# All activations begin 64 bytes further on in each partition

## The chip, the cores and the metric

The kernel runs on 1 core of a Trainium2 chip. Its time is the device time of that core in microseconds, the median of several runs. Each core has a matrix engine (TensorE, in the profile PE, with its weight loads as PEld), a vector engine (DVE), a scalar engine (ACT), GpSimd (POOL) and a queue engine (SP), with one on-chip memory of 128 partitions between them.

## The reference

Two blocks follow each other on 256 tokens of width 2048. What matters here is that nearly all of it is products of activations with large weight matrices, in float32:

```python
def first_block(...):                      # two layers
    xm_l = x_lat * (1.0 + sc_l) + sh_l     # shift and scale from a small product with cond
    proj = xm @ w_in                       # layer 0: q, k, v, o, z_m, gates, u_p, z_p
    ...                                    # mLSTM scan, pooling
    x_lat = layer_norm(ALPHA * x_lat + g_l * (y_l @ w_out_even[j]), ...)
    u, v, z = jnp.split(xm @ w_in, 3, axis=-1)      # layer 1, and y_l @ w_out_odd

def second_block(...):
    c_q, c_kv, k_r, x_r, y_r, ga, gr = split_columns(n @ w_in[l])
    ...                                    # attention, recurrent branch, each with its output product
    h = h + (g_attn * y_attn + g_rnn * y_rnn) @ w_out[l]
    h = h + peer_ffn(...)                  # 16,384 experts
    gate = jax.nn.sigmoid(rms_norm(h, ple_norm[l]) @ w_ple_gate[l])
    h = h + gate * (p[l] @ w_ple_proj[l])
    return rms_norm(h, final_norm)
```

The experts (`peer_u`, `peer_v`, 16,384 x 2048 each) are not gathered: the kernel multiplies with all of them and picks by one-hot products.

## The kernel before, in words

All weights stream from memory in 669 units of 128 partitions x 2048 floats (8 KB in each partition) through a ring of four buffers. ACT rounds each half of a unit to the reduced form fp32r (`unit_hi`, line 1102); POOL (line 478), or DVE in some stages (lines 1659, 1775, 2414), writes the rest, ring minus `unit_hi`, to `unit_lo`. The activations are split in the same way into a hi and a lo tile (`xl`, `xc`, `y`, `cn`, `o`, `ry`, `mix`, `w_r`, `p_r`). A product is then three matmuls: weights hi with activation hi, weights hi with activation lo, weights lo with activation hi.

Most of them stand in `n_unit` (line 541): the stationary operand is a 128x128 piece of a unit's half, the moving operand 256 columns of one activation tile. The same triple stands in `two_units` (513), for both sets of tokens (696), in the experts' second product (1055, activations `w_r`) and in the last projection (1078). In `v1_tokens` (593) and `o_tokens` (570) the roles are exchanged: 128 columns of the activation are stationary, 512 columns of a unit's half move. In lines 673 and 675, too, a unit's half moves, against a stationary operand of only 4 or 2 columns (`cond_parts`).

The chip's own scheduling sets no order here: every engine runs a program written by hand, with semaphores between them. SP loads units in order, each when its ring buffer is free. ACT, then POOL or DVE, then PE follow at most four halves apart (`NBUF = 4`).

On-chip memory is laid out by hand as well. First come, one behind the other and each rounded up to 64 bytes, the fixed tiles: the ring, four `unit_hi`, four `unit_lo` of 4,096 bytes in each partition, the residual `h`, vectors, constants (`con`), rows. Ahead of the zones they take 91,584 bytes from the first, `base0`. Everything else is placed by `zone(name, kb, ...)` at `z0` plus a number of KB: all the split activations, and nearly all other intermediate tiles. A few zones lie 64 bytes or a multiple of that beside a whole KB (`q0` at 98.0625 KB and `u_pad`'s neighbours at 106.0625 KB among them). The change is in the line that sets `z0`.

The operand addresses that follow, modulo 512 bytes and counted from `base0`: every buffer of the weights' halves starts at 0, and every 128-column piece of it too. The split activations start at 448. `con` starts at 320.

Of the kernel before, what the change touches and what calls it, by code (L numbers as in the profile page):

```python
# [190 lines left out]
def program(nc, A, out):  # L191
    with ExitStack() as ctx:
        base0 = (nc.sbuf_base + 63) // 64 * 64
        at = [base0]
# [4 lines left out]
        def fixed(name, shape, dt):  # L199
            t = place(name, shape, dt, at[0])  # L200
            at[0] += (int(np.prod(shape[1:])) * 4 + 63) // 64 * 64
            return t
# [12 lines left out]
        rstd = fixed("rstd", [P, T], F32)  # L215
        tick = fixed("tick", [1, 1], F32)
        lam_s = fixed("lam_s", [P, KC], F32)
        z0 = (at[0] + 63) // 64 * 64
        KB = 1024

        def zone(name, kb, shape, dt=F32):
# [2559 lines left out]
```

## Time and profile before

| | |
|---|---|
| median of 3 runs | 3753.03 us (3751.19 to 3781.72) |
| the profiled execution's own time | 3763.23 us |
| its span, first to last instruction | 3761.4 us |
| PE busy | 3610.3 us, 96% of the span |
| PEld busy | 3481.5 us, 93% |
| DVE, POOL, ACT busy | 2091.6, 2039.0, 1562.3 us |
| granted TensorE clock, mean | 0.98 |

The profiled execution is 10.2 us above the median of the runs and inside their spread. A busy PE says only that some matmul was in the array: the next one is fed before the last one has left, so that one lasts about 276 ns while a new one begins every 113 ns. How fast PE goes is read from the distance of the starts: first and last start of a group, divided by the number of matmuls between them.

### The profile page before, as it was taken

To read this page: it belongs to the slowest core of one execution; us is meant where nothing else is said; L and a number is where in the kernel's file an instruction comes from. 1 tells how busy PE (TensorE), PEld (TensorE's weight loads), DVE (VectorE), ACT (ScalarE), POOL (GpSimd) and SP (SyncE) were. 2 spreads that over 40 slices of the span, in tenths; PEclk is the share of its full clock that TensorE was granted. 3 is DMA by queue.
4 is the path that set the end of the run, shared out by engine and by line. 5 is a ranking of instruction groups with operands and counts; after the bars stand their busy time and mean duration, and the time that the engine had idled before them with its cause. 6 is when DMAs were issued, how large, how long until landed. Compare 5 with 4: busy or idle time off the path is not lost.

```text
span 3761.4 us, 71588 instructions
## 1 busy us (share of the span) xinstructions
PE 3610.3 (96%) x30016; PEld 3481.5 (93%) x30016; DVE 2091.6 (56%) x3062; ACT 1562.3 (42%) x1970; POOL 2039.0 (54%) x816
## 2 busy tenths in 40 slices
PE   6999998999999889999999999999999999999998
PEld 3799897979999879999999999999999999999998
DVE  6686456783724465554114679784444666544454
ACT  5413433334344334454444434434444444444453
POOL 0147591008084648789899960007888100188876
PEclk9999999999999999999999999999999999999999
DMA  8557751765653424545455545545555455455543
GB/s 330 191 210 261 277 221 73 299 234 189 251 200 132 147 100 157 180 157 185 175 200 192 192 182 185 179 169 184 196 190 192 179 179 183 180 196 190 192 166 124
DMA packets 98407, 716.37 MB, mean 190 GB/s; under 512 B 11040, under 2 KB 11168, under 8 KB 12064
## 3 DMA queue, kind: packets, MB, share of 16 engines
q1 hardware_dynamic: 97056, 703.65, 51.0%
q10 hardware_dynamic: 1152, 9.87, 0.7%
q8 instruction: 148, 2.42, 0.3%
q14 instruction: 51, 0.42, 0.0%
HBM read 711.38 MB, written 2.10 MB: 190 GB/s over the span
## 4 chain that ended last, share of the span: by engine, by line
PE 83%; DVE 8%; POOL 4%; DMA 2%; ACT 2%; issue 2%; DVEq 0%; SPq 0%; POOLq 0%; ACTq 0%
PE bank L541 54%; PE bank L1055 19%; POOL unit_lo L478 3%; DMA ring<-in_w 2%; PE bank L593 2%; PE bank L696 2%; DVE unit_lo L1775 1%; PE bank L570 1%; PE bank L1006 1%; ACT unit_hi L1102 1%; PE bank L635 1%; PE bank L513 1%; DVE ada_acc L1576 1%; PE bank L805 1%; DVE unit_lo L1659 1%
## 5 line engine op out<-in xcount | busy, mean ns | idle before, releaser
L478 POOL TENSOR_TENSOR unit_lo<-ring,unit_hi 128x1024 fp32r<-128x1024 f32 x806 | 2023.2, 2525 | 1656.7 <-ACT unit_hi L1102 1655.2
L1102 ACT ACTIVATE unit_hi<-ring 128x1024 fp32r<-128x1024 f32 x1204 | 1239.7, 1056 | 1194.7 <-PE bank L541 479.5
L541 PE MATMUL bank<-xl_hi,unit_hi 128*128 128x256 f32 x4688 | 1321.6, 282 | 23.2 <-POOL unit_lo L478 9.9
L541 PE MATMUL bank<-xl_lo,unit_hi 128*128 128x256 f32 x4688 | 1307.5, 279 | 0.0
L541 PE MATMUL bank<-xl_hi,unit_lo 128*128 128x256 f32 x4688 | 1307.0, 279 | 0.0
L541 PEld LDWEIGHTS bank<-xl_hi,unit_hi 128*128 128x128 f32 x4688 | 890.5, 190 | 30.5 <-issue 11.5
L541 PEld LDWEIGHTS bank<-xl_hi,unit_lo 128*128 128x128 f32 x4688 | 888.0, 189 | 0.0
L541 PEld LDWEIGHTS bank<-xl_lo,unit_hi 128*128 128x128 f32 x4688 | 886.8, 189 | 0.6
L1055 PE MATMUL bank<-w_r,unit_hi 128*128 128x256 f32 x4096 | 699.7, 277 | 4.0 <-DVE w_r L2584 4.0
L1055 PEld LDWEIGHTS bank<-w_r,unit_hi 128*128 128x128 f32 x4096 | 619.1, 188 | 4.3 <-issue 4.3
L1055 PE MATMUL bank<-w_r,unit_lo 128*128 128x256 f32 x2048 | 566.8, 277 | 0.0
L2584 DVE TENSOR_TENSOR w_r<-peer_w,w_r 128x256 fp32r<-128x256 f32 x128 | 290.0, 2266 | 398.2 <-ACT w_r L1471 397.6
L1055 PEld LDWEIGHTS bank<-w_r,unit_lo 128*128 128x128 f32 x2048 | 386.0, 188 | 0.0
L2414 DVE TENSOR_TENSOR unit_lo<-ring,unit_hi 128x1024 fp32r<-128x1024 f32 x224 | 265.4, 1220 | 54.9 <-ACT unit_hi L1102 54.6
L1576 DVE SCALAR_TENSOR_TENSOR ada_acc<-ring,cond,ada_acc 128x2048 f32<-128x2048 f32 x64 | 185.5, 2899 | 29.7 <-DMA ring<-in_w 28.7
L1659 DVE TENSOR_TENSOR unit_lo<-ring,unit_hi 128x1024 fp32r<-128x1024 f32 x102 | 120.5, 1221 | 72.6 <-ACT unit_hi L1102 58.5
L1452 ACT ACTIVATE peer_w<-bank 128x248 f32<-128x248 f32 (+30 forms) x87 | 24.3, 279 | 304.4 <-PE bank L541 304.4
L541 PE MATMUL bank<-ry_hi,unit_hi 128*128 128x256 f32 x480 | 132.8, 277 | 0.6 <-issue 0.6
L541 PE MATMUL bank<-ry_lo,unit_hi 128*128 128x256 f32 x480 | 132.5, 276 | 0.0
L541 PE MATMUL bank<-ry_hi,unit_lo 128*128 128x256 f32 x480 | 132.5, 276 | 0.0
L541 PE MATMUL bank<-xc_hi,unit_hi 128*128 128x256 f32 x448 | 126.3, 282 | 0.6 <-ACT ple_in L1495 0.6
L541 PE MATMUL bank<-xc_lo,unit_hi 128*128 128x256 f32 x448 | 125.7, 281 | 0.0
(441 smaller groups left out, 5135.0 us busy)
## 6 DMA issues: line engine op xcount, KB each, us to landing
ring<-in_w SPq DMA_DIRECT2D x669, 1024.0 KB, 4.8
resid<-in_xT ACTq DMA_DIRECT2D x1, 2048.0 KB, 15.7
tmp_ctx<-in_ctxT ACTq DMA_DIRECT2D x1, 2048.0 KB, 11.3
sgu_rows<-in_sgr ACTq DMA_DIRECT2D x1, 2048.0 KB, 9.5
rnn_gates<-in_rgw ACTq DMA_DIRECT2D x1, 2048.0 KB, 8.8
out<-resid SPq DMA_DIRECT2D x4, 512.0 KB, 2.6
con<-in_con ACTq DMA_DIRECT2D x1, 512.0 KB, 3.3
con<-in_con ACTq DMA_DIRECT2D x1, 448.0 KB, 7.9
```

Source lines behind the costliest of these rows:

```text
L478: pool.tensor_tensor(lb[b][:], ring[slot][:, f * HALF:(f + 1) * HALF], hb[b][:].bitcast(F32), ALU.subtract).then_inc(lo_done, 1)
L513: mm = pe.matmul(bank[(s.t0 + j) % TILES][:, 0:T], w[b][:, (k % 8) * P:(k % 8 + 1) * P], mv[x][:, k, :], start=(k == 0 and w is hb and x = ...
L541: mm = pe.matmul(bank[(s.t0 + tile[m]) % TILES][:, 0:T], w[b][:, (i % 8) * P:(i % 8 + 1) * P], mv[x][:, k, :], start=(k == 0 and w is hb a ...
L570: mm = pe.matmul(bank[(s.t0 + 2 * (j // 4) + t) % TILES][:], xl[x][:, k, t * P:(t + 1) * P], w_[u][:, q * 512:(q + 1) * 512], start=(k == ...
L593: mm = pe.matmul(bank[(s.t0 + 2 * block + t) % TILES][:], xl[x][:, k, t * P:(t + 1) * P], w_[u][:, q * 512:(q + 1) * 512], start=(k == 0 a ...
L696: mm = pe.matmul(dst[:, m * T:(m + 1) * T], w_[b][:, (i % 8) * P:(i % 8 + 1) * P], mv[x][:, k, :], start=(first and w_ is w[0] and x == 0 ...
L1055: mm = pe.matmul(o, w_[b][:, c * P:(c + 1) * P], wr[j % 2][:, x, :], start=(first and j == 0 and cc % 2 == 0 and w_ is hb and x == 0), sto ...
L1102: act.activation(hb[b][:], ring[slot][:, f * HALF:(f + 1) * HALF], ACT.Copy).then_inc(hi_done, 1)
L1576: dve.scalar_tensor_tensor(a[:], ring[u % RING][:], col, a[:], ALU.mult, ALU.add).then_inc(plain_done, 1)
L1659: dve.tensor_tensor(lb[b][:], ring[(s.u0 + s.npos[j]) % RING][:, f * HALF:(f + 1) * HALF], hb[b][:].bitcast(F32), ALU.subtract).then_inc(l ...
L2414: dve.tensor_tensor(lb[b][:], ring[(s.u0 + u) % RING][:, f * HALF:(f + 1) * HALF], hb[b][:].bitcast(F32), ALU.subtract).then_inc(lo_done, 1)
L2584: dve.tensor_tensor(wr[j % 2][:, 1, :], at(W, i), wr[j % 2][:, 0, :].bitcast(F32), ALU.subtract).then_inc(S("wr_ready"), 1)
```

## The change

`z0`, the place from which all zones are counted, was rounded up to 64 bytes. It is now rounded up to a multiple of 512 bytes counted from `base0`. By the sizes of the fixed tiles, 91,584 becomes 91,648 bytes from `base0`: 64 bytes further. Every zone moves by these 64 bytes; rings, halves of units, residual, vectors and constants stay. No instruction, wait or order is changed.

```diff
         tick = fixed("tick", [1, 1], F32)
         lam_s = fixed("lam_s", [P, KC], F32)
-        z0 = (at[0] + 63) // 64 * 64
+        z0 = (at[0] - base0 + 511) // 512 * 512 + base0
         KB = 1024
 
         def zone(name, kb, shape, dt=F32):
             off = z0 + int(kb * KB)
```

## Rows read from the trace of the kernel before

**Rows 1.** The page: busy time, share of the span, instructions of each engine.

```profile
PE 3610.3 (96%) x30016; PEld 3481.5 (93%) x30016; DVE 2091.6 (56%) x3062; ACT 1562.3 (42%) x1970; POOL 2039.0 (54%) x816
```

**Rows 2.** The page: shares of the chain that ended last, by engine and by line.

```profile
PE 83%; DVE 8%; POOL 4%; DMA 2%; ACT 2%; issue 2%; DVEq 0%; SPq 0%; POOLq 0%; ACTq 0%
PE bank L541 54%; PE bank L1055 19%; POOL unit_lo L478 3%; DMA ring<-in_w 2%; PE bank L593 2%; PE bank L696 2%; DVE unit_lo L1775 1%; PE bank L570 1%; PE bank L1006 1%; ACT unit_hi L1102 1%; PE bank L635 1%; PE bank L513 1%; DVE ada_acc L1576 1%; PE bank L805 1%; DVE unit_lo L1659 1%
```

**Rows 3.** PE's groups by line and form: busy us, mean ns of one, idle before.

```profile
L541 PE MATMUL bank<-xl_hi,unit_hi 128*128 128x256 f32 x4688 | 1321.6, 282 | 23.2 <-POOL unit_lo L478 9.9 <-DVE unit_lo L1659 5.4 <-issue 2.8
...
L1055 PE MATMUL bank<-w_r,unit_hi 128*128 128x256 f32 x4096 | 699.7, 277 | 4.0 <-DVE w_r L2584 4.0
L1055 PE MATMUL bank<-w_r,unit_lo 128*128 128x256 f32 x2048 | 566.8, 277 | 0.0
...
L541 PE MATMUL bank<-xc_hi,unit_hi 128*128 128x256 f32 x448 | 126.3, 282 | 0.6 <-ACT ple_in L1495 0.6
```

**Rows 4.** Line 1055, window 2600:2700: ns min/median/max, first and last start.

```profile
L1055 PE MATMUL bank<-w_r,unit_hi x589: 276/276/276, 2599.9 to 2699.9; 128*128 128x256 f32 x197
L1055 PE MATMUL bank<-w_r,unit_lo x295: 276/276/276, 2599.8 to 2699.8; 128*128 128x256 f32 x148
```

**Rows 5.** Line 541, window 2240:2340, the same columns.

```profile
L541 PE MATMUL bank<-xl_lo,unit_hi x284: 281/281/281, 2239.8 to 2339.8; 128*128 128x256 f32 x142
L541 PE MATMUL bank<-xl_hi,unit_lo x284: 281/281/281, 2240.0 to 2339.9; 128*128 128x256 f32 x142
L541 PE MATMUL bank<-xl_hi,unit_hi x283: 281/281/281, 2240.1 to 2339.7; 128*128 128x256 f32 x142
```

**Rows 6.** PE in order of time about 2380: start us, us, what.

```profile
2379.28 0.28 PE L541 MATMUL bank<-xl_hi,unit_hi 128*128 128x256 f32 x1
2379.40 0.28 PE L541 MATMUL bank<-xl_lo,unit_hi 128*128 128x256 f32 x1
2379.52 0.28 PE L541 MATMUL bank<-xl_hi,unit_lo 128*128 128x256 f32 x1
2379.64 0.82 PE L988 MATMUL bank<-con,peer_g 128*128 128x128 f32 x6
2380.21 0.37 PE L541 MATMUL bank<-xl_hi,unit_hi 128*128 128x256 f32 x1
...
2380.77 0.28 PE L541 MATMUL bank<-xl_lo,unit_hi 128*128 128x256 f32 x1
2380.88 0.28 PE L541 MATMUL bank<-xl_hi,unit_lo 128*128 128x256 f32 x1
2380.99 0.28 PE L541 MATMUL bank<-xl_hi,unit_hi 128*128 128x256 f32 x1
```

**Rows 7.** Line 541 in seven stretches: window, length, PE busy, clock, DMA.

```profile
333.20:376.00 42.80, 42.80 (x366) 1.00 0.59 222
...
1732.20:1811.00 78.80, 78.80 (x671) 1.00 0.54 193
2176.10:2379.00 202.90, 202.89 (x1723) 1.00 0.53 192
3658.80:3743.00 84.20, 84.20 (x717) 1.00 0.38 137
sum 498.20, PE 498.19; mean PE 71.17
```

**Rows 8.** Line 593, window 800:840; columns as in rows 4.

```profile
L593 PE MATMUL bank<-unit_hi,xl_lo x59: 388/388/394, 799.7 to 839.5; 128*128 128x512 f32 x59
L593 PE MATMUL bank<-unit_lo,xl_hi x59: 392/392/394, 799.9 to 839.8; 128*128 128x512 f32 x59
L593 PE MATMUL bank<-unit_hi,xl_hi x58: 388/390/392, 800.4 to 839.1; 128*128 128x512 f32 x58
```

**Rows 9.** Lines 673 and 675 in order of time, columns as in rows 6.

```profile
81.36 0.39 PE L673 MATMUL bank<-unit_hi,cond_parts 128*4 128x512 f32 x1
...
82.98 0.39 PE L675 MATMUL bank<-unit_lo,cond_parts 128*2 128x512 f32 x1
```

**Rows 10.** Plain f32 matmuls of lines 635, 652 and 958, windows of 25, 8, 1 us.

```profile
L635 PE MATMUL bank<-ln_sq,con x32: 379/379/379, 743.1 to 749.8; 128*128 128x256 f32 x32
...
L652 PE MATMUL bank<-con x38: 379/379/379, 750.0 to 758.0; 128*128 128x256 f32 x38
...
L958 PE MATMUL bank<-x_conv,rnn_gates x4: 377/378/379, 1542.1 to 1542.7; 128*128 128x256 f32 x4
```

**Rows 11.** Every engine in two stretches: PE, PEld, DVE, ACT, POOL, clock, DMA.

```profile
2240.00:2340.00 100.00, 100.00 (x851) 100.00 (x851) 92.74 (x172) 40.20 (x52) 0.00 (x0) 1.00 0.53 189
2600.00:2700.00 100.00, 100.00 (x884) 100.00 (x884) 42.80 (x19) 44.58 (x56) 88.18 (x38) 1.00 0.54 197
```

## The prediction

> **What bounds the kernel now.** I read the engines' shares first: PE is busy 96% of the span, DVE 56%, POOL 54%, ACT 42% [rows 1]. The chain of waits agrees: 83% of it is PE, 54% of the span in line 541 and 19% in line 1055 [rows 2]. Both lines feed 256 columns of a split activation against a 128x128 piece of a unit's half. PE hardly waits: the 4,688 matmuls of the first group have 23.2 us of idle time before them in all [rows 3]. So the time is the number of these matmuls times the distance of their starts. In the profile's list by line and form, line 541 has three groups for each activation, with 4,688, 480, 448, 272, 256, 256 and 224 matmuls each: 3 x 6,624 = 19,872. Line 1055 has 4,096 + 2,048 = 6,144 [rows 3]. Together 26,016. One nanosecond more or less for each is 26 us, 0.7%.
>
> **Two distances.** In the window from 2600, line 1055 begins 884 matmuls from 2599.8 to 2699.9: 100.1 / 883 = 113.4 ns [rows 4]. In the window from 2240, line 541 begins 851 from 2239.8 to 2339.9: 100.1 / 850 = 117.8 ns, and each one lasts 281 instead of 276 ns [rows 5]. The granted clock is 1.00, the 2.4 GHz level, in both [rows 11], so it isn't the clock. Nor is it the operands: about 2380 the same line with the same tiles changes from 0.12 us to 0.11 us a step, with six f32 matmuls of line 988 between [rows 6]. The long distance is a way in which the stream settles after an interruption, and stays. It fills seven long stretches of 498.2 us in sum [rows 7]; shorter ones I leave out. At the short distance these would take 498.2 x (1 - 113.4/117.8) = 18.6 us less.
>
> At one column for each cycle of 2.4 GHz, 256 columns take 106.7 ns. Something therefore adds 6.7 ns to a matmul at the short distance and 11.1 ns at the long one, in all about 6.7 x 26,016 + 18.6 = 193 us. That is what a better place of the operands could win at the very most, and the question of this change.
>
> **The change part by part.** It removes and adds no instruction, on no engine or queue. It moves every zone by 64 bytes. For a matmul of line 541 or 1055 the moving operand starts at 448 modulo 512 bytes from the weights' halves before, and at 0 after; its stationary operand stays at 0. What that costs no row shows directly, so I bound it by the nearest ones.
>
> - A moving operand that starts at 0 is there already: in line 593 a unit's half moves, 512 columns of it. 176 matmuls begin from 799.7 to 839.8: 40.1 / 175 = 229 ns, 114.6 ns for 256 columns [rows 8]. That lies between the two distances of line 541. Starting the moving stream on the 512-byte multiple wins nothing there.
> - The fetch of the stationary operand doesn't cause the stall: with 4 or 2 stationary columns the eight matmuls of lines 673 and 675 begin from 81.36 to 82.98, 1.62 / 7 = 231 ns apart for 512 columns [rows 9], as slow as with 128. A collision between the two fetches, which is what their relative place would set, should be far smaller there.
> - Two operands at the same place modulo 512 are there too, in plain f32. Line 652 takes both from `con` (difference 0), 8.0 / 37 = 216 ns apart; line 958 takes both from zones a whole number of KB apart (difference 0), 0.6 / 3 = 0.20 us with one digit; line 635 has 128 bytes of difference, 6.7 / 31 = 216 ns [rows 10]. No difference between 0 and 128. But f32 needs 216 ns for its 256 columns, so that its fetch has more time than that of fp32r.
>
> So the three rows that come nearest all say: no change. From both sides: below, the stall could go down by a step as large as the one between the two distances (4.4 ns), above it could grow by one. 4.4 x 26,016 = 114.5 us. I take 0, because rows 8 have fp32r, the place after the change and the same speed, and keep both ends for the range.
>
> The Trainium skill, "SBUF — State Buffer", section "Who interferes with whom", has TensorE with one read port for the moving operand and one for weight loads, independent of each other and of all engines; by that rule a relative place costs nothing, and the sum stays at 0. Its "Specifications (TRN2)" give lines of 16 bytes, which a shift of 64 leaves as they were. The rule "Back-to-back issue gap" in "TensorE: Matmul & The Clock Gate" gives N/2.4 + 2.5 = 109.2 ns for 256 columns. The trace disagrees: it shows 113.4 ns; by the rule, a stall of 4.2 ns is there to be removed, which would be 109 us.
>
> The other engines: the zones' 64 bytes also move what ACT, DVE and POOL write and read. The split of a unit (ring, `unit_hi`, `unit_lo`) doesn't move, and that is POOL's and most of ACT's work. POOL, 88% busy in the experts' second product, and DVE, 93% in the stretch from 2240 [rows 11], are covered by a PE that is full in both. I cost them at nothing. If PE went to 109.0 ns, POOL would be at 88.2 x 113.4 / 109.0 = 92%: still cover, but little in it. Five DMAs go into zones, against 669 into the ring.
>
> **Sum:** 3763.2 + 0. The profiled execution is 10.2 us above the median of the runs, so the forecast for the median is 3753 us. How often the stream settles at the long distance is chance in part: none of these stretches would take 18.6 us off, twice as many would add as much. The likeliest case's own range is 3725 to 3785.
>
> **The rivals.**
> - *A collision: slower.* Both fetches now start on the same multiple of 512 bytes. If the memory is laid out in banks that repeat with 512 bytes, the load of the next weights and the moving stream ask for the same bank, and the long distance becomes the only one. Place: every triple of lines 541 and 1055. Price: 114.5 for one step more on all, less the 18.6 already paid: +96, 3849 us for the median. It decides from 1.5 ns a matmul on (38 us). For it: that there are two levels at all, with the same operands, tells of something that two streams share. Against it: rows 8 to 10. Chance 0.18, and 0.04 for other losses, of a smaller or a larger step.
> - *The stall goes: faster.* If the stall comes from the difference of 64 bytes between the two operands (448 against 0), equal places take it away: 109.0 instead of 113.4 ns, and no long stretches. -114.5 - 18.6 = -133, 3620 us for the median. For it: line 593 also has a difference of 64 bytes, the other way, and stalls as well; f32 with differences of 0 and 128 doesn't show one. Against it: lines 673 and 675 stall with `cond_parts`, whose pieces start 16 bytes apart and so at many differences. Chance 0.17, and 0.05 for half of that, 3686 us.
> - *The long stretches alone vanish:* -18.6, 3734 us. Inside 1%. Chance 0.10.
> - *The change doesn't do what it says:* if `base0` itself isn't at a multiple of 512, the zones are aligned with the units but not in absolute terms. Then only the relative place has changed, and if the absolute one is what counts, the effect is as good as any other shift of 64 bytes. I count it in the forecast.
>
> **How the numbers follow.** Forecast (no change) 0.46, long stretches gone 0.10; together 0.56 within 1%. One per cent, 37.5 us, is about what a measurement of this kernel tells from no change. Faster by over 1%: 0.17 + 0.05 = 0.22. Slower by over 1%: 0.18 + 0.04 = 0.22. The range goes from 3650, which takes in half a step down but leaves out the whole one, to 3855, which takes in the whole step up: 0.17 below and about 0.02 above are left out. The likeliest time stays 3753.
>
> **What would show it.** If I am right, line 1055 in the experts' second product still begins every 113.4 ns and lasts 276 ns, line 541 shows 113.4 and 117.8 in other stretches, line 593 still takes 229 ns. A collision would show 281 ns or more in line 1055, where there is not one such matmul in rows 4 now. A stall that goes would show distances near 109 ns and a POOL above 90% there. Wrong from the start would be the use of line 593 as a measure for line 541, if the two read the memory in different ways, and the belief that ACT's, DVE's and POOL's work on zones doesn't feel the place.

## The result, and the profile after

The changed kernel takes 3887.78 us (median of 4 runs, 3886.17 to 3888.91) against 3763.3 us for the kernel before (median of 4 runs, the three of the table above and one more; 3751.19 to 3781.72): ratio 1.0326, 95% interval 1.0275 to 1.0377. It is slower by 3.3%, and the forecast of no change and its range (3650 to 3855) are both missed. The spans of the profiled executions are 3887.1 and 3761.4 us, 125.7 us apart.

The page after, engines first, then PE's groups in the columns of [rows 3]:

```profile
PE 3744.4 (96%) x30016; PEld 3620.4 (93%) x30016; DVE 2058.8 (53%) x3062; ACT 1559.7 (40%) x1970; POOL 2029.4 (52%) x816
...
L541 PE MATMUL bank<-xl_hi,unit_hi 128*128 128x256 f32 x4688 | 1343.9, 287 | 16.1 <-POOL unit_lo L478 5.4
L541 PE MATMUL bank<-xl_lo,unit_hi 128*128 128x256 f32 x4688 | 1331.7, 284 | 0.0
```

```profile
L1055 PE MATMUL bank<-w_r,unit_hi 128*128 128x256 f32 x4096 | 738.9, 283 | 4.0 <-DVE w_r L2584 4.0
L1055 PE MATMUL bank<-w_r,unit_lo 128*128 128x256 f32 x2048 | 580.5, 283 | 0.0
```

PE is busy 134.1 us longer with the same 30,016 instructions and idle 8.4 us less (142.7 against 151.1): 125.7, the whole difference. DVE, ACT and POOL are busy no longer than before, against [rows 1]. Line 1055's matmuls last 283 ns where they lasted 277.

The distance of the starts, line 1055 in the window 2650:2750, line 541 in 2300:2380, then line 635 (f32), then line 593 in 820:849; columns as in [rows 4]:

```profile
L1055 PE MATMUL bank<-w_r,unit_hi x557: 280/283/287, 2649.8 to 2749.9; 128*128 128x256 f32 x186
L1055 PE MATMUL bank<-w_r,unit_lo x278: 280/283/287, 2649.9 to 2749.7; 128*128 128x256 f32 x139
```

```profile
L541 PE MATMUL bank<-xl_hi,unit_hi x223: 283/283/283, 2299.8 to 2379.7; 128*128 128x256 f32 x112
L541 PE MATMUL bank<-xl_lo,unit_hi x223: 283/283/283, 2299.9 to 2379.8; 128*128 128x256 f32 x112
L541 PE MATMUL bank<-xl_hi,unit_lo x223: 283/283/283, 2300.0 to 2379.9; 128*128 128x256 f32 x112
```

```profile
L635 PE MATMUL bank<-ln_sq,con x32: 379/379/379, 754.0 to 760.7; 128*128 128x256 f32 x32
```

```profile
L593 PE MATMUL bank<-unit_hi,xl_lo x44: 389/389/389, 819.9 to 848.7; 128*128 128x512 f32 x44
L593 PE MATMUL bank<-unit_hi,xl_hi x43: 389/389/389, 819.6 to 848.2; 128*128 128x512 f32 x43
L593 PE MATMUL bank<-unit_lo,xl_hi x43: 389/389/389, 820.3 to 848.9; 128*128 128x512 f32 x43
```

Line 1055: 835 matmuls in 100.1 us, 100.1 / 834 = 120.0 ns, where [rows 4] have 113.4. Line 541: 669 matmuls in 80.1 us, 80.1 / 668 = 119.9 ns, where [rows 5] have 117.8 and [rows 4], for the same form, 113.4. Line 635: 6.7 / 31 = 216 ns, as in [rows 10]. Line 593: 130 matmuls in 29.3 us, 29.3 / 129 = 227 ns against 229 in [rows 8]: with the roles exchanged and 512 columns, the new place is a little better.

Line 541 and all other engines, in the columns of [rows 11]:

```profile
2300.00:2400.00 100.00, 100.00 (x836) 100.00 (x835) 91.40 (x165) 41.29 (x54) 0.00 (x0) 1.00 0.50 178
2650.00:2750.00 100.00, 100.00 (x835) 100.00 (x835) 40.05 (x18) 42.51 (x53) 83.25 (x36) 1.00 0.53 187
```

The granted clock is 1.00 as before, and in both stretches 835 or 836 matmuls fit where 851 and 884 did. PE is full in both; nobody keeps it waiting there. The fp32r matmuls of 256 columns have become slower by themselves, and the two distances of before have become one of 120 ns.

### The profile page after: what moved, and what is told of

It reads as the page before. It is cut to its first block, busy times and chain, and to the rows that moved or that the text cites. A ratio compares the mean times of both kernels' runs of the same rounds, so it can differ in the third digit from the quotient of the medians.

```text
span 3887.1 us, 71588 instructions
## 1 busy us (share of the span) xinstructions
PE 3744.4 (96%) x30016; PEld 3620.4 (93%) x30016; DVE 2058.8 (53%) x3062; ACT 1559.7 (40%) x1970; POOL 2029.4 (52%) x816
## 4 chain that ended last, share of the span: by engine, by line
PE 83%; DVE 9%; POOL 3%; DMA 2%; ACT 2%; issue 1%; SPq 0%; DVEq 0%; POOLq 0%; ACTq 0%
PE bank L541 54%; PE bank L1055 19%; POOL unit_lo L478 3%; DMA ring<-in_w 2%; PE bank L593 2%; PE bank L696 2%; DVE ada_acc L1576 1%; DVE unit_lo L1775 1%; PE bank L570 1%; PE bank L1006 1%; ACT unit_hi L1102 1%; PE bank L513 1%; PE bank L635 1%; DVE unit_lo L1659 1%; PE bank L805 0%
## 5 line engine op out<-in xcount | busy, mean ns | idle before, releaser
L541 PE MATMUL bank<-xl_hi,unit_hi 128*128 128x256 f32 x4688 | 1343.9, 287 | 16.1 <-POOL unit_lo L478 5.4
L541 PE MATMUL bank<-xl_lo,unit_hi 128*128 128x256 f32 x4688 | 1331.7, 284 | 0.0
L541 PE MATMUL bank<-xl_hi,unit_lo 128*128 128x256 f32 x4688 | 1331.4, 284 | 0.0
L541 PEld LDWEIGHTS bank<-xl_hi,unit_hi 128*128 128x128 f32 x4688 | 904.7, 193 | 22.4 <-issue 10.8
L541 PEld LDWEIGHTS bank<-xl_lo,unit_hi 128*128 128x128 f32 x4688 | 904.9, 193 | 0.5
L541 PEld LDWEIGHTS bank<-xl_hi,unit_lo 128*128 128x128 f32 x4688 | 904.4, 193 | 0.0
L1055 PE MATMUL bank<-w_r,unit_hi 128*128 128x256 f32 x4096 | 738.9, 283 | 4.0 <-DVE w_r L2584 4.0
L1055 PEld LDWEIGHTS bank<-w_r,unit_hi 128*128 128x128 f32 x4096 | 636.7, 191 | 4.3 <-issue 4.3
L1055 PE MATMUL bank<-w_r,unit_lo 128*128 128x256 f32 x2048 | 580.5, 283 | 0.0
```

The lines of the kernel that those rows point to most:

```text
L541: mm = pe.matmul(bank[(s.t0 + tile[m]) % TILES][:, 0:T], w[b][:, (i % 8) * P:(i % 8 + 1) * P], mv[x][:, k, :], start=(k == 0 and w is hb a ...
L1055: mm = pe.matmul(o, w_[b][:, c * P:(c + 1) * P], wr[j % 2][:, x, :], start=(first and j == 0 and cc % 2 == 0 and w_ is hb and x == 0), sto ...
```

## The experiments

Below, *difference* is the start of the moving operand less that of the stationary one in line 1055 and 541, modulo 512 bytes: 448 before, 0 after. e1, e2, e3 and g1 are medians of several executions; all others are single ones, set beside the kernel before on the same chip. Executions of the kernel before go from 3747 to 3805 us, so the single ones are judged by the distance in line 1055, not by the time. Where no other window is named it is 2650:2750, and the rows' columns are those of [rows 4].

**Is it the activations' own place, or the place relative to the weights?** Three kernels. In e1 and e2 `h` and small fixed tiles are taken from behind the halves and put ahead of `unit_hi`, which moves the halves (`vec` and `con` move too); in e3 only the two `w_r` move:

```diff
 e1_units448 (activations stay, halves move: difference 0)
         ring = [fixed(f"ring{i}", [P, UNIT], F32) for i in range(RING)]
+        h = fixed("resid", [P, KC, T], F32)
+        mod = fixed("mod", [P, 96, 2], F32)
+        cond = fixed("cond", [P, KC, 2], F32)
+        tick = fixed("tick", [1, 1], F32)
         hb = [fixed(f"unit_hi{i}", [P, HALF], F32R) for i in range(NBUF)]
 e2_both64 (h and tick ahead of the halves, and:)
+        z0 = (at[0] + 63) // 64 * 64 + 64
 e3_wr64
-        wr = [zone(f"w_r{i}", 100 + 2 * i, [P, 2, T], F32R) for i in range(2)]
+        wr = [zone(f"w_r{i}", 100.0625 + 2 * i, [P, 2, T], F32R) for i in range(2)]
```

> All activations stay where they are in the kernel before; instead the eight buffers of the weights' halves (unit_hi, unit_lo) lie 448 bytes further modulo 512, so that moving and stationary operand of lines 541 and 1055 again start at the same place modulo 512. Theory R (the place of the moving operand relative to the stationary one counts): starts 120.0 ns apart in lines 541 and 1055, no 113.4, line 593 near 227 ns, about 3885 us. Theory A (the moving operand's own place counts): the activations haven't moved, so 113.4 and 117.8 ns as before, 3750 to 3785 us. Theory O (ACT, DVE and POOL are slower on the moved zones): as A.

> Activations 64 bytes further as in the change, and the weights' halves 64 bytes further too: the difference of the two is 448 modulo 512 as in the kernel before, the activations' own place is that of the change. Theory R: 113.4 and 117.8 ns, 3750 to 3785 us. Theory A: 120.0 ns, about 3888 us. Theory O: about 3888 us, with 113.4 ns in line 1055 and the time lost elsewhere.

> Kernel before, with only the two buffers w_r (the moving operand of line 1055, 6144 matmuls) 64 bytes further. Theories R and A: line 1055 goes from 113.4 to 120.0 ns, everything else keeps 113.4 and 117.8; 6144 x 6.6 ns = 40.6 us more, about 3800 us. Theory O: line 1055 keeps 113.4 ns and the time stays within 10 us of before.

- e1: 3896.2 us, ratio 1.0324 (1.0279 to 1.0369). The activations lie where they lay, and the whole loss is there.
- e2: 3762.35 us, ratio 0.9999 (0.9971 to 1.0026). The activations lie where the change put them, and nothing is lost.
- e3: 3802.01 us, ratio 1.0089 (1.0058 to 1.012), 36 us over the 3765.83 of before in the same job, where 40.6 were expected from line 1055 alone.

Line 1055 in e1, e2, e3:

```profile
L1055 PE MATMUL bank<-w_r,unit_hi x557: 283/283/283, 2649.8 to 2749.9; 128*128 128x256 f32 x186
L1055 PE MATMUL bank<-w_r,unit_lo x278: 283/283/283, 2650.1 to 2749.8; 128*128 128x256 f32 x139
```

```profile
L1055 PE MATMUL bank<-w_r,unit_hi x589: 276/276/276, 2649.8 to 2749.8; 128*128 128x256 f32 x197
L1055 PE MATMUL bank<-w_r,unit_lo x295: 276/276/276, 2649.9 to 2749.9; 128*128 128x256 f32 x148
```

```profile
L1055 PE MATMUL bank<-w_r,unit_hi x557: 283/283/283, 2649.8 to 2749.9; 128*128 128x256 f32 x186
L1055 PE MATMUL bank<-w_r,unit_lo x278: 283/283/283, 2649.9 to 2749.6; 128*128 128x256 f32 x139
```

120.0 ns (100.1 / 834), 113.4 ns (100.1 / 883), 120.0 ns. The relative place decides; theories A and O are out.

**Which differences are good?** The halves moved by other amounts, activations as before (e4 to e8: `h` and tiles of 64, 128, 192, 256 and 320 bytes modulo 512 ahead of `unit_hi`), and two with steps of 32 bytes:

```diff
 e4_units64                      e5_units128
+        tick = fixed(...)       +        cond = fixed(...)
 e6_units192                     e7_units256
+        cond = ..., tick = ...  +        mod = fixed(...)
 e8_units320                     e11_zones32
+        mod = ..., tick = ...   +        z0 = (at[0] + 63) // 64 * 64 + 32
 e12_diff160 (cond ahead of the halves, and:)
+        z0 = (at[0] + 63) // 64 * 64 + 96
```

> The weights' halves 64 bytes further, activations as before: the moving operand starts at 384 modulo 512 from the stationary one, a place that no run has shown. Theory R with a bank that repeats every 512 bytes: the distance is one of a small set (109, 113.4, 117.8, 120.0 ns), not that of before in all stretches; if two fetches only collide when they start together, 113.4 or less everywhere, 3740 us or less. Theory A: 113.4 and 117.8 as before.

> The weights' halves 128 bytes further, activations as before: the moving operand starts at 320 modulo 512 from the stationary one. So far 448 gives 113.3 and 117.8 ns (114.7 ns in the mean), 0 gives 120.0 and 384 gives 118.8 in the mean. Theory R1 (the two fetches go round the same banks of 64 bytes with a period of 512; the weight load begins late and half-way through the moving stream, and only some differences let both pass): the mean here differs from 118.8 and 114.7 by over 1 ns. Theory R2 (448 is a special place since there the moving stream is one bank behind; all others collide): about 119 to 120 ns, 3855 to 3890 us.

> The weights' halves 192 bytes further: difference 256 modulo 512, half the supposed period, farthest from the start of the other fetch. Theory R1: a different distance again, perhaps the lowest, since the fetches of a period of 512 are farthest apart here (109 to 113.4 ns, 3630 to 3750 us). Theory R2: 119 to 120 ns, 3855 to 3890 us. If the period is 256 instead of 512, the same as difference 0: 120.0 ns and 3890 us.

> The weights' halves 256 bytes further: difference 192 modulo 512. Theory R1: its own distance. With a period of 256 the same as 448: 113.3 and 117.8 ns and 3750 to 3785 us. Theory R2: 119 to 120 ns, 3855 to 3890 us.

> The weights' halves 320 bytes further: difference 128 modulo 512. Theory R1: its own distance. With a period of 256 the same as 384: 118.8 ns and 3855 us. With a period of 128 the same as 0: 120.0 ns and 3890 us. Theory R2: 119 to 120 ns, 3855 to 3890 us.

> Kernel before with all zones only 32 bytes further: difference 480, 224 modulo 256, between 192 (113.3 and 117.8 ns) and 0 (120.0 ns). If banks are 64 bytes wide, half of each piece is in the next bank: a distance between 114 and 120 ns, 3760 to 3890 us. If 32 bytes shift the stream in time by half a bank, a distance outside the set so far (for example 116.7 or 110 ns).

> Weights' halves 128 bytes and zones 96 bytes further: difference 416, 160 modulo 256, between 128 (118.7 ns) and 192 (113.3 and 117.8 ns). If 192 is the middle of a good region, about 113 to 118 ns and 3740 to 3850 us; if it is the region's edge on this side and 224 is good, this one is near 118.7 ns. Faster than before only if the settled distance falls below 113.3 ns or the 117.8 ns stretches vanish: 3740 us or less.

| run | difference | modulo 256 | line 1055, ns | time, us (before on the same chip) |
|---|---|---|---|---|
| after | 0 | 0 | 120.0 | 3887.78 (3763.3) |
| e6 | 256 | 0 | 120.0 | 3893.59 (3780.14) |
| e5 | 320 | 64 | 117.8 | 3832.07 (3780.14) |
| e4 | 384 | 128 | 118.6 | 3854.92 (3765.83) |
| e8 | 128 | 128 | 118.6 | 3854.66 (3780.14) |
| e12 | 416 | 160 | 118.6 | 3853.55 (3804.97) |
| before | 448 | 192 | 113.4 | |
| e7 | 192 | 192 | 113.4 | 3748.44 (3780.14) |
| e11 | 480 | 224 | 118.3 | 3849.22 (3804.97) |

In the last column before is a single execution, but for the first row and e4, where it is a median. Two pairs and the place of before repeat with 256 bytes, to the digit of the view. The rows of e5, e7 and e6 are the pattern:

```profile
L1055 PE MATMUL bank<-w_r,unit_hi x568: 279/279/279, 2649.8 to 2749.9; 128*128 128x256 f32 x190
L1055 PE MATMUL bank<-w_r,unit_lo x283: 280/280/280, 2650.1 to 2749.7; 128*128 128x256 f32 x142
```

```profile
L1055 PE MATMUL bank<-w_r,unit_hi x590: 276/276/276, 2649.9 to 2750.0; 128*128 128x256 f32 x197
L1055 PE MATMUL bank<-w_r,unit_lo x295: 276/276/276, 2649.8 to 2749.7; 128*128 128x256 f32 x148
```

```profile
L1055 PE MATMUL bank<-w_r,unit_hi x557: 283/283/283, 2649.8 to 2749.9; 128*128 128x256 f32 x186
L1055 PE MATMUL bank<-w_r,unit_lo x278: 283/283/283, 2650.0 to 2749.8; 128*128 128x256 f32 x139
```

Of the six places tried modulo 256 only 192 gives 113.4 ns; 32 bytes to either side cost 5 ns. The kernel before had the good one. That e6, half of 512 away, might be best was wrong: it is the changed kernel again. R1's period was wrong (256, not 512), and R2 fails by e7, which is as good as before, and by e5 (117.8 ns, 3832 us, where it said 119 to 120). e12 came out at what had been named for 192 as the edge of a good region, but by e11 that region doesn't go on to 224: 192 is good by itself.

The table is of line 1055, and 192 isn't the only place with more than one distance. In e12 line 541 goes at two within 100 us, at the same clock (windows 2040:2080 and 2140:2180, columns as in [rows 11]):

```profile
2040.00:2080.00 40.00, 40.00 (x336) 40.00 (x335) 16.96 (x38) 16.43 (x17) 36.27 (x16) 1.00 0.55 195
2140.00:2180.00 40.00, 40.00 (x343) 40.00 (x343) 32.12 (x24) 17.14 (x17) 39.49 (x16) 1.00 0.58 207
```

That is 120.0 and 117.5 ns by the starts; e4's line 541 has stretches at 118.7 and at 120.0 ns. Line 593, with the roles exchanged, answers to the place in another way: here e5 with its 126 matmuls in 29.2 us (29.2 / 125 = 234 ns, against 229 before and 227 after):

```profile
L593 PE MATMUL bank<-unit_hi,xl_hi x42: 393/396/398, 819.7 to 848.0; 128*128 128x512 f32 x42
L593 PE MATMUL bank<-unit_hi,xl_lo x42: 393/396/398, 820.2 to 848.4; 128*128 128x512 f32 x42
L593 PE MATMUL bank<-unit_lo,xl_hi x42: 393/396/398, 820.7 to 848.9; 128*128 128x512 f32 x42
```

**Does the size of the weight load matter?** Line 1055 with fewer stationary columns:

```diff
 e9_thin_448, e10_thin_0 (e10 and f4 with z0 64 bytes further)
-  mm = pe.matmul(o, w_[b][:, c * P:(c + 1) * P], wr[j % 2][:, x, :],
+  mm = pe.matmul(o[0:4, :], w_[b][:, c * P:c * P + 4], wr[j % 2][:, x, :],
 f4_m64_0
+  mm = pe.matmul(o[0:64, :], w_[b][:, c * P:c * P + 64], wr[j % 2][:, x, :],
```

> The kernel before (difference 448, which the runs so far show to be the same as 192 modulo 256), with only 4 instead of 128 stationary columns in line 1055: the weight load shrinks, the moving stream stays. 124 of 128 columns of the experts' second product are left out. If the two fetches collide, line 1055 no longer depends on the place: the same distance as in the next run, 109 to 114 ns. If the moving stream alone is limited, 113.3 ns stay.

> The changed kernel (difference 0) with the same 4 stationary columns in line 1055, with 124 of 128 columns of that product left out. Collision of the two fetches: line 1055 falls from 120.0 ns to that of the run before this one (109 to 114 ns), about 40 us less than 3888. If the weight load has no part in it, 120.0 ns stay.

> The changed kernel (difference 0) with 64 instead of 128 stationary columns in line 1055, half of the columns of that product are left out. 128 columns gave 120.0 ns, 4 columns 113.3 ns. If the loss grows with the length of the weight load: about 116.7 ns. If one meeting of the two fetches is enough: 120.0 ns. If only the load's end matters, 113.3 ns.

Line 1055 in e9, e10, f4:

```profile
L1055 PE MATMUL bank<-w_r,unit_hi x572: 277/278/279, 2649.9 to 2749.8; 128*4 128x256 f32 x191
L1055 PE MATMUL bank<-w_r,unit_lo x287: 277/279/279, 2649.8 to 2749.9; 128*4 128x256 f32 x144
```

```profile
L1055 PE MATMUL bank<-w_r,unit_hi x590: 276/276/276, 2649.8 to 2750.0; 128*4 128x256 f32 x197
L1055 PE MATMUL bank<-w_r,unit_lo x295: 276/276/276, 2649.9 to 2749.9; 128*4 128x256 f32 x148
```

```profile
L1055 PE MATMUL bank<-w_r,unit_hi x590: 276/276/276, 2649.7 to 2749.8; 128*64 128x256 f32 x197
L1055 PE MATMUL bank<-w_r,unit_lo x295: 276/276/276, 2650.0 to 2749.9; 128*64 128x256 f32 x148
```

At difference 0, 64 columns and 4 columns (both 100.2 / 884 = 113.3 ns) take the loss away; 128 columns have it. At 448, 4 columns cost 100.1 / 858 = 116.7 ns, more than 128 do. A plain collision, where less to load is never worse, doesn't give that. The times were 3775.91 us (e9) and 3842.4 us (e10), with 3804.97 for before on that chip, and 3846.1 us (f4), with 3767.74.

So the number of stationary columns counts, and by e1 and e2 the place of the stationary operand does. Whether it is the second half of the load that does the harm at difference 0 isn't shown: with fewer stationary columns the output has fewer partitions too (`o[0:64]`, `o[0:4]`), and no run changes one without the other. Line 1055 loses 6,144 x 6.6 = 41 us at difference 0 and line 541 most of the rest; the fewer columns were tried in line 1055 alone, and line 541 stayed at 120.0 ns in e10 and f4.

**Does each matmul answer to the load beside it?** Only `unit_lo` moved, `cond` or `tick` or both put between `unit_hi` and `unit_lo` (with this `h`, `vec` and `con` move by as much):

```diff
         hb = [fixed(f"unit_hi{i}", [P, HALF], F32R) for i in range(NBUF)]
+        cond = fixed("cond", [P, KC, 2], F32)      # f2, g1; tick: f1; both: f3
         lb = [fixed(f"unit_lo{i}", [P, HALF], F32R) for i in range(NBUF)]
```

> Only unit_lo lies 64 bytes further: difference 448 for the two matmuls with unit_hi, 384 (128 modulo 256) for the one with unit_lo. Theory N (a moving stream collides with the load of the next weights, which runs beside it): only the start behind xl_lo x unit_hi moves away, the two others keep 113.3 ns; mean (2 x 113.3 + 118.7) / 3 = 115.1 ns. Theory M (the three streams settle together): all three distances change, mean not 115.1. The 117.8 ns stretches stay in both. About 3770 to 3830 us. A version without any 117.8 ns would be faster than before: 3735 us.

> Only unit_lo lies 128 bytes further: difference 320 (64 modulo 256) for the matmul with unit_lo. Theory N: mean (2 x 113.3 + 117.8) / 3 = 114.8 ns, the long step behind xl_lo x unit_hi. Theory M: another mean, all three steps changed. About 3770 to 3830 us; faster than before only if the 117.8 ns stretches go.

> Only unit_lo lies 192 bytes further: difference 256 (0 modulo 256) for the matmul with unit_lo. Theory N: mean (2 x 113.3 + 120.0) / 3 = 115.6 ns with 120.0 only behind xl_lo x unit_hi, about 3790 us. If its own weights count instead of the next ones, 120.0 only behind xl_hi x unit_lo. Theory M: another mean.

> The arrangement of f2 (unit_lo alone 128 bytes further, everything else as before) timed against the kernel before. If its single time of 3733 us was no accident, the median is 3725 to 3740 us, 0.5 to 1.2% below before, with less spread than before, since the stretches at 117.8 ns, whose number changes from run to run, are gone. If it was chance (a run with few such stretches), the median is 3750 to 3770.

Line 1055 in f1, f2, f3:

```profile
L1055 PE MATMUL bank<-w_r,unit_hi x566: 279/282/286, 2649.8 to 2750.0; 128*128 128x256 f32 x189
L1055 PE MATMUL bank<-w_r,unit_lo x282: 277/280/281, 2650.1 to 2749.7; 128*128 128x256 f32 x141
```

```profile
L1055 PE MATMUL bank<-w_r,unit_hi x590: 276/276/276, 2649.9 to 2750.0; 128*128 128x256 f32 x197
L1055 PE MATMUL bank<-w_r,unit_lo x295: 276/276/276, 2649.8 to 2749.8; 128*128 128x256 f32 x148
```

```profile
L1055 PE MATMUL bank<-w_r,unit_hi x547: 282/283/290, 2649.8 to 2749.9; 128*128 128x256 f32 x183
L1055 PE MATMUL bank<-w_r,unit_lo x273: 282/283/283, 2650.0 to 2749.8; 128*128 128x256 f32 x137
```

118.3, 113.3 and 122.2 ns, where theory N said 115.1, 114.8 and 115.6. For f3 the 122.2 ns are only the first of the two rounds of line 1055; in the second, from 3378 us on, it goes at 117.8 (windows 2650:2750 and 3550:3650, columns as in [rows 11]):

```profile
2650.00:2750.00 100.00, 100.00 (x820) 100.00 (x819) 40.38 (x18) 41.54 (x52) 83.57 (x35) 1.00 0.50 178
3550.00:3650.00 100.00, 100.00 (x851) 100.00 (x850) 41.68 (x18) 43.10 (x54) 86.74 (x36) 1.00 0.52 188
```

N falls in all three, by either value of f3. In the window from 2650 the three steps of a triple, by the starts in the trace, are about 116, 119 and 120 ns in f1 and 118, 122 and 127 ns in f3, against 113 to 114 before: all three change there, as theory M said, though `unit_lo` alone has moved. In f2 none changes (113 to 114), which M did not say either. So the triple doesn't come apart into three independent pairs; M names that and doesn't forecast a distance. The times of f1 and f3 were 3839.15 and 3873.18 us, both above what had been expected. f2 took 3732.67 us against 3767.74, below what had been expected. Timed, g1 takes **3736.26 us** (11 runs, 3731.93 to 3739.8) against 3762.66 (16 runs, 3747.45 to 3801.11): ratio 0.9914, 0.9885 to 0.9942. Its page and line 541 in 2200:2280:

```profile
PE 3583.0 (96%) x30016; PEld 3454.4 (92%) x30016; DVE 2094.2 (56%) x3062; ACT 1561.8 (42%) x1970; POOL 2042.5 (55%) x816
...
L541 PE MATMUL bank<-xl_lo,unit_hi 128*128 128x256 f32 x4688 | 1302.0, 278 | 0.0
```

```profile
L541 PE MATMUL bank<-xl_hi,unit_lo x231: 275/277/284, 2199.8 to 2279.9; 128*128 128x256 f32 x116
L541 PE MATMUL bank<-xl_hi,unit_hi x230: 275/277/384, 2199.9 to 2279.7; 128*128 128x256 f32 x115
```

In that stage, where [rows 5] last 281 ns, they now last 277. PE is busy 27.3 us less than before; the prediction had reckoned 18.6 us for the seven long stretches and left out the shorter ones. By 0.9%, with an interval that leaves out 1, g1 is faster than the kernel before.

## Why the prediction was wrong, point by point

- **What bounds the kernel** was right: 26,016 matmuls, a nanosecond of each worth 26 us, and all that changed is that distance. 6.6 x 26,016 = 171.7 us less the 27.3 us which the long stretches had cost before (by g1) gives 144.4; PE is busy 134.1 longer. Added up from the starts in the two traces, line 541 takes 99.8 us more and line 1055 39.2; what makes up the rest isn't resolved. PE's idle time became 8.4 us shorter.
- **The step that failed** is "A moving operand that starts at 0 is there already", line 593 as the measure for the change, and with it the 0 in the sum. Line 593's moving operand starts at 0, but its stationary one started at 448: its difference was 64, not 0. The prediction knew this difference, for it counts it in favour of its rival of a stall that goes, and didn't apply it here. By e1 and e2 the moving operand's own start has no effect, so rows 8 said nothing on difference 0. What stood there in place of the 0 was 6.6 ns for each matmul: 120.0 ns in line 1055 instead of 113.4. There was no row with fp32r and difference 0, and the sum should have said so. In line 593 itself, with roles and columns exchanged, the effect even has the other sign: 229 to 227 ns.
- **"The fetch of the stationary operand doesn't cause the stall"**, from 4 and 2 columns in [rows 9], was wrong as an inference. e1 and e2 show that the stationary operand's place has its part, e10 that with 4 columns the loss at difference 0 is gone, and e9 that 4 columns are slower than 128 at 448, for a reason that stays open. A slow stream with a small load doesn't acquit the large one.
- **The f32 rows** [rows 10] were read rightly and don't carry over: 216 ns before and after. The prediction named the doubt, that f32 has more time, and gave it too little weight.
- **The other engines at nothing**: right. DVE, ACT and POOL are busy as long or less, and e2 has the new place of all zones at a ratio of 0.9999. For the ports between engines, as the Trainium skill has them in "SBUF — State Buffer", "Who interferes with whom", that is no contradiction. The word "independent", which it has for TensorE's own two read ports, doesn't hold as the prediction used it: by that rule e1 should have cost nothing, and it cost 3.2%. The 109.2 ns from "TensorE: Matmul & The Clock Gate", "Back-to-back issue gap", in the Trainium skill, were reached by no arrangement; the shortest fp32r distance that any run settled at is 113.3 ns. The prediction used that formula wrongly: the section gives it for an isolated matmul and says that in a stream of loads and matmuls both set the spacing. A stall of 4.2 ns "by the rule" doesn't follow from it.
- **The rival of the collision** had the place and the sign, at 0.18. Its size was too small: I took the step between the two distances of before (4.4 ns) for the next one, and it was 6.6 ns from the short one, where 113.4 became 120.0 and not 117.8. Its 3849 us would have been 3753 + 171.7 - 18.6 = 3906, the measured time is 3888, and the range ended at 3855. Its period of 512 bytes is 256, and a plain collision isn't the mechanism.
- **The stall goes** (3620 us) happened nowhere. **The long stretches vanish** happened, in g1, through another place, and was worth 0.9% (0.6 to 1.2%), somewhat more than the 18.6 us, 0.5%, put on it.

What stays open is how the fetches share the memory: why the loss at difference 0 needs more than 64 stationary columns, why 4 columns are worse than 128 at 448, what sets the several distances of one place, and where the rest above the 106.7 ns comes from with which the prediction reckons. The runs give the table, not the circuit.

## What to carry to other kernels

Where a stream of matmuls with a new stationary operand each is the bound and no engine keeps it waiting, read the distance of the starts in each stage; two values at the same clock are a reason to try the relative place of moving and stationary operands in steps of 64 bytes. Aligning both to the same round number was the worst uniform place tried here for 128 stationary and 256 moving columns, and better than the others tried for line 593, where 512 move (227 ns against 229 to 234): each shape wants its own look. Count such a shift as a change to every matmul, and look for a row with the same difference of both operands, not with the same start of one.

## What the runs showed of the hardware that was not expected

- By line 1055, for fp32r, 128 stationary and 256 moving columns, the distance depends on the difference of the two starts modulo 256 bytes: 120.0 ns at 0, 117.8 at 64, 118.6 at 128 and 160, 113.4 at 192, 118.3 at 224. Three pairs 256 bytes apart agree.
- One stream can go at two distances with the same operands at the same clock: 113.4 and 117.8 ns in line 541 at difference 192, 117.5 and 120.0 at 160 (e12), 122.2 and 117.8 in line 1055 of f3. Executions of the kernel before went from 3747 to 3801 us in one job; with `unit_lo` 128 bytes further they lay within 8 us. That the share of the long stretches makes this spread is likely but not shown: of the kernel before one execution alone has a trace.
- Fewer stationary columns can be slower: 116.7 ns with 4 (e9) against 113.4 with 128, at 448.
- Plain f32 matmuls don't react at all: 216 ns in line 635 of every kernel.
